# Filter stage with its sum and difference first and half the one-column products; two norms with the gate product ahead of the root, output written in halves

## What is computed

```python
def rmsnorm_2(x, g):
    return x * rsqrt(mean(x * x) + 1e-6) * g
def ffn_half(s, shift, scale, gate, g_pre, g_post, w_in, w_out):
    h = swiglu_2(modulate(rmsnorm_2(s, g_pre), shift, scale), w_in, w_out)
    return s + 0.5 * gate * rmsnorm_2(h, g_post)
# hyena_kernel, L = 256
h = h @ w4
h_fwd, h_bwd = split(h, 2)
h_fwd, h_bwd = h_fwd * decay, h_bwd * decay
k = concat([h_fwd, zeros, h_bwd[:0:-1]])
return k / (sum(abs(k), axis=0) + 1e-6)
# bidir_long_conv
y = irfft(rfft(u, 2 * L) * rfft(k, 2 * L))[:L]
# second_block
xs = ffn_half(xs, ...)
y = token_mixer(hx, ...)
xs = xs + mod_x[5] * rmsnorm_2(y, g[3])
return ffn_half(xs, ...)
```

## Time and profile before

| | |
|---|---|
| three executions | 2611.27, 2613.20, 2613.49 us |
| profiled execution, its own time | 2607.8 us |
| its span in the trace | 2606.0 us |
| mean granted clock of TensorE | 0.987 |
| TensorE busy | 2511.2 us (96%) |
| VectorE busy | 1811.8 us (70%) |
| ScalarE busy | 1451.3 us (56%) |
| share of TensorE in the chain that ended last | 84% |

### The profile page before, as it was taken

The page is one execution under the profiler, slowest core; times in us unless marked ns, Lnnn a source line. Parts: engine busy times, 40 slices in busy tenths (PEclk is TensorE's granted clock), DMA queues, the critical chain, the costliest instruction groups (busy, mean ns, idle before and its releaser), DMA issues.

```text
span 2606.0 us, 33172 instructions
## 1 busy us (share of the span) xinstructions
PE 2511.2 (96%) x11783; PEld 1992.0 (76%) x11783; DVE 1811.8 (70%) x1759; ACT 1451.3 (56%) x1613; POOL 67.0 (3%) x54
## 2 busy tenths in 40 slices
PE   7989999989999999999999999999999999998998
PEld 6668887667888888888888777888874787777787
DVE  6555446558999998989898985655544575777554
ACT  4553434547777777777777775435332333466443
POOL 0000000011000000000000000600000000000000
PEclk9999999989999999999999999999999999999999
DMA  6885552759999999999999996655534334435651
GB/s 218 308 285 189 192 178 81 266 175 378 394 373 358 370 364 367 354 375 347 381 351 377 340 342 204 232 183 187 184 129 138 101 126 146 125 104 172 203 190 65
DMA packets 330622, 642.13 MB, mean 246 GB/s; under 512 B 14408, under 2 KB 113256, under 8 KB 330344
## 3 DMA queue, kind: packets, MB, share of 16 engines
q1 hardware_dynamic: 327800, 631.02, 69.6%
q0 software_dynamic: 2736, 9.96, 1.0%
HBM read 633.07 MB, written 7.86 MB: 246 GB/s over the span
## 4 chain that ended last, share of the span: by engine, by line
PE 84%; DVE 7%; ACT 4%; issue 3%; DMA 1%; POOL 0%; SPq 0%; DVEq 0%; ACTq 0%; POOLq 0%
PE ps L926 19%; PE ps L852 19%; PE ps L956 10%; PE ps L881 10%; PE ps L1335 6%; PE ps L786 5%; PE ps L1362 2%; PE ps L1267 2%; DVE As L2343 1%; PE ps L1070 1%; ACT As L1736 1%; PE ps L865 1%; PE ps L941 1%; PE ps L1326 1%; DVE ringL L2313 1%
## 5 line engine op out<-in xcount | busy, mean ns | idle before, releaser
L2343 DVE TENSOR_TENSOR As<-ringA,As 128x2048 fp32r<-128x2048 f32 x318 | 733.7, 2308 | 220.3 <-ACT As L1653 132.4
L926 PE MATMUL ps<-As,xgs 128*128 128x512 f32 x2688 | 660.4, 395 | 6.4 <-DVE As L2343 3.8
L926 PEld LDWEIGHTS ps<-As,xgs 128*128 128x128 f32 x2688 | 494.7, 188 | 112.7 <-issue 5.7
L1736 ACT ACTIVATE As<-ringA 128x2048 fp32r<-128x2048 f32 x224 | 428.7, 1914 | 29.9 <-PE ps L926 27.6
L852 PE MATMUL ps<-As,xs 128*128 128x512 f32 x1456 | 376.0, 396 | 3.9 <-DVE hh L2380 3.9
L956 PE MATMUL ps<-Bs,hds 128*128 128x512 f32 x1332 | 323.4, 391 | 5.0 <-DVE hds L2406 2.2
L852 PEld LDWEIGHTS ps<-As,xs 128*128 128x128 f32 x1456 | 273.0, 190 | 63.4 <-DVE hh L2380 4.8
L956 PEld LDWEIGHTS ps<-Bs,hds 128*128 128x128 f32 x1332 | 248.0, 188 | 64.2 <-issue 11.0
L2425 DVE TENSOR_TENSOR Bs<-ringB,Bs 128x2048 fp32r<-128x2048 f32 x111 | 254.1, 2289 | 7.7 <-ACT Bs L1766 5.2
L1766 ACT ACTIVATE Bs<-ringB 128x2048 fp32r<-128x2048 f32 x111 | 213.2, 1921 | 63.0 <-PE ps L956 62.3
L881 PE MATMUL ps<-Bs,hds 128*128 128x512 f32 x1056 | 247.9, 390 | 0.0
(11 more groups left out here) (399 smaller groups left out, 3246.0 us busy)
## 6 DMA issues: line engine op xcount, KB each, us to landing
ringA<-in_moe_w_gate SPq DMA_DIRECT2D x112, 1024.0 KB, 5.9
ringA<-in_moe_w_up SPq DMA_DIRECT2D x112, 1024.0 KB, 6.1
ringB<-in_moe_w_down SPq DMA_DIRECT2D x112, 1024.0 KB, 6.1
ringA<-in_w_ff_in SPq DMA_DIRECT2D x132, 512.0 KB, 4.7
ringA<-in_w_in SPq DMA_DIRECT2D x56, 1024.0 KB, 5.3
ringA<-in_w_ada SPq DMA_DIRECT2D x36, 1024.0 KB, 6.4
ringB<-in_w_ff_out SPq DMA_DIRECT2D x33, 1024.0 KB, 5.0
ringA<-in_dense_w_gate SPq DMA_DIRECT2D x28, 512.0 KB, 3.6
```

Of the source, the lines that this page charges most:

```text
L926: m = mm(ps[:, bank, :], lhs(l, tt, k), As[:, h, r, k % 4, :], start=k == 0 and n == 0, stop=k == KC - 1 and n == 2)
L1736: A(As[:, h, 0, :, :], ringA[:, (p["a"] + u) % 2, 4 * h:4 * h + 4, :], ACT.Copy).then_inc(A_high, 1)
L2343: V.tensor_tensor(As[:, h, 1, :, :], ringA[:, (p["a"] + u) % 2, 4 * h:4 * h + 4, :], f32(As[:, h, 0, :, :]), ALU.subtract).then_inc(A_spli ...
```

## The change

**Filter stage.** For tile 0 nothing changes. For tile 1 VectorE makes the sum (into `decay`) and the difference (into `ha[:, 1]`) right after `hs` and `hd`, and counts up `f_h` after each; the copy (L2909) falls away, the absolute values come after. TensorE goes to the transform at `f_h` = 2 (groups 4 to 7, which read the difference, at 3). The absolute values of both tiles are added on VectorE into `hs[:, 1]` between its copies 5 and 9, so the column sums are 8 one-column products in the place of 16, and they stand behind the transform. `rn` is read then; the second block of `z` waits for that. `late_high` and `weight_low` of the first block of `z` move between the copies.

**Norm after `wo`.** The product of each half with the gate (`mixed_gate`) is made as soon as that half is squared, without the reciprocal; one fused pass `x = xn * rr + x` (`mixed_add`) follows the root. For tile 1 that pass stands ahead of `split_rows(0)`.

**The end.** The last `down` finishes the first 512 columns of a tile ahead of the second (`down_halves`). Squares, gate products, final passes and output DMAs go by halves of 512 columns.

```diff
@@ SyncE
             for tt in range(TILES):
-                sp.wait_ge(x_out, tt + 1)
-                sp.dma_start(out[tt * P:(tt + 1) * P, :], x[:, tt, :]).then_inc(out_done, 16)
-            sp.wait_ge(out_done, 32)
+                for half in range(2):
+                    c = slice(half * BW, (half + 1) * BW)
+                    sp.wait_ge(x_out, 2 * tt + half + 1)
+                    sp.dma_start(out[tt * P:(tt + 1) * P, c], x[:, tt, c]).then_inc(out_done, 16)
+            sp.wait_ge(out_done, 64)
@@ TensorE
+                def down_halves(i, u, weights):
+                    for tt in range(T):
+                        pe.wait_ge(hdT_ready, ffn_count(p, T, e, i, u, tt))
...
+                        for half in range(2):
+                            for q in range(2):
+                                for n, (l, r) in enumerate(((0, 0), (0, 1), (1, 0))):
+                                    m = mm(ps[:, 4 + 2 * tt + half, :], hds[:, tt, l, q, :], weights[r][:, q, half * 512:(half + 1) * 512],
...
+                            m.then_inc(down_done if half else acc_half, 1)
...
             pe.wait_ge(f_h, 2)
-            for c in range(KC):
-                for tt in range(TILES):
-                    last = mm(ps[:, 3, c:c + 1], ha[:, tt, c * P:(c + 1) * P], ones[:, 0:1], start=tt == 0, stop=tt == TILES - 1)
-            last.then_inc(rn_mm, 1)
...
             for q in range(10):
                 fc, half = q // 2, q % 2
-                src = hd if fc in (2, 3) else hs
+                src = (hd[:, 0, :], ha[:, 1, :]) if fc in (2, 3) else (hs[:, 0, :], decay)
                 if q >= 4:
                     pe.wait_ge(k_copied, q - 3)
+                if q == 4:
+                    pe.wait_ge(f_h, 3)
...
+            pe.wait_ge(f_h, 4)
+            for c in range(KC):
+                last = mm(ps[:, 3, c:c + 1], hs[:, 1, c * P:(c + 1) * P], ones[:, 0:1], start=True, stop=True)
+            last.then_inc(rn_mm, 1)
             pe.wait_ge(k_copied, 10)
...
             for n in range(6):
+                if n == 1:
+                    pe.wait_ge(rn_read, 1)
@@ ScalarE
-            for h in range(2):
-                late_high(ph["z"], 0, h)
             for q in range(0, 10, 2):
...
                 A(KF[:, q // 2, 0:512], ps[:, 4 + q % 4, :], ACT.Copy).then_inc(k_copied, 1)
+                if q < 4:
+                    late_high(ph["z"], 0, q // 2)
...
             for tt in range(TILES):
+                act.wait_ge(acc_half, tt + 1)
+                A(fnrow[:, 0:BW], ps[:, 4 + 2 * tt, :], ACT.Square, accum_out=ss[:, tt:tt + 1]).then_inc(squared, 1)
+                act.wait_ge(squared, 2 * TILES + 2 * tt + 1)
+                ch.done(A(std[:, 2 + tt:3 + tt], ss[:, tt:tt + 1], ACT.Identity, scale=1.0 / D, bias=epsc[1e-6]))
                 act.wait_ge(down_done, ph["ff1"]["s"] + 2 * NB2 - 1 + tt)
-                ch.done(A(xn[:, tt, :], ps[:, 4 + 2 * tt:6 + 2 * tt, :].rearrange("p a b -> p (a b)"), ACT.Square, accum_out=ss[:, tt:tt + 1]))
-                A(std[:, tt:tt + 1], ss[:, tt:tt + 1], ACT.Sqrt, bias=epsc[1e-6], scale=1.0 / D).then_inc(fin_std, 1)
+                A(fnrow[:, 0:BW], ps[:, 5 + 2 * tt, :], ACT.Square, accum_out=ss[:, 2 + tt:3 + tt]).then_inc(squared, 1)
+                act.wait_ge(squared, 2 * TILES + 2 * tt + 2)
+                A(std[:, tt:tt + 1], ss[:, 2 + tt:3 + tt], ACT.Sqrt, bias=std[:, 2 + tt:3 + tt], scale=1.0 / D).then_inc(fin_std, 1)
@@ VectorE
+                if tt:
+                    V.tensor_tensor(decay, hs[:, 1, :], hd[:, 1, :], ALU.add).then_inc(f_h, 1)
+                    V.tensor_tensor(ha[:, 1, :], hs[:, 1, :], hd[:, 1, :], ALU.subtract).then_inc(f_h, 1)
+                    continue
...
+            for q in range(1, 10, 2):
+                wait((k_mm, q + 1), (k_copied, q))
+                V.tensor_copy(KF[:, q // 2, 512:D], ps[:, 4 + q % 4, :]).then_inc(k_copied, 1)
+                if q < 4:
+                    weight_low(ph["z"], 0, q // 2)
+                if q == 5:
+                    ch.done(V.tensor_tensor(hs[:, 1, :], hs[:, 1, :], hd[:, 1, :], ALU.add))
+                if q == 7:
+                    V.tensor_tensor(hs[:, 1, :], hs[:, 1, :], ha[:, 0, :], ALU.add).then_inc(f_h, 1)
...
-            mixed_out(0)
+            for n in range(2):
+                mixed_gate(0, n)
             mixed_add(0)
+            mixed_gate(1, 0)
             tile_scale("ff1", 0, x, 1)
             plain_rows(0)
-            mixed_out(1)
+            mixed_gate(1, 1)
+            mixed_add(1)
             split_rows(0)
-            mixed_add(1)
             A_parts(ph["ff1"], 0, 0, 0, 1)
...
             for tt in range(TILES):
+                for half in range(2):
+                    c = slice(half * BW, (half + 1) * BW)
+                    dve.wait_ge(squared, 2 * TILES + 2 * tt + half + 1)
+                    V.tensor_tensor(xn[:, tt, c], ps[:, 4 + 2 * tt + half, :], gateG[:, 3, c], ALU.mult).then_inc(gated, 1)
                 dve.wait_ge(fin_std, tt + 1)
                 ch.done(V.reciprocal(rr[:, tt:tt + 1], std[:, tt:tt + 1]))
-                ch.done(V.scalar_tensor_tensor(xn[:, tt, :], acc(tt), rr[:, tt:tt + 1], gateG[:, 3, :], ALU.mult, ALU.mult))
-                V.tensor_tensor(x[:, tt, :], x[:, tt, :], xn[:, tt, :], ALU.add).then_inc(x_out, 1)
+                for half in range(2):
+                    c = slice(half * BW, (half + 1) * BW)
+                    dve.wait_ge(gated, 2 * TILES + 2 * tt + half + 1)
+                    V.scalar_tensor_tensor(x[:, tt, c], xn[:, tt, c], rr[:, tt:tt + 1], x[:, tt, c], ALU.mult, ALU.add).then_inc(x_out, 1)
```

More of the change, by code:

```diff
@@ L813, in project, with feed @@
                         between()
-            def feed(p, lhs, T, e=0, ready=None, xsm=None, after=None, head=1, leads=True, drains=True, rows=None, turns_free=None):
+            def feed(p, lhs, T, e=0, ready=None, xsm=None, after=None, head=1, leads=True, drains=True, rows=None, turns_free=None, halves=False):
                 nb = p["nb"]
@@ L900, in body @@
                         down(*prev, tts=(1,))
-                        down(i, u, weights=down_home(p, p["b"] + u))
+                        (down_halves if halves else down)(i, u, weights=down_home(p, p["b"] + u))
                     elif not lead:
@@ L1510, in _ @@
                 turn_rows("ff1", 0, hf)
-            feed(ph["ff1"], split_stream, 2, rows="ff1")
+            feed(ph["ff1"], split_stream, 2, rows="ff1", halves=True)
         @block.gpsimd
@@ L2909, in _ @@
                 V.tensor_copy(hs[:, tt, :], decay).then_inc(f_h, 1)
+            wait((f_h, 3))
+            V.scalar_tensor_tensor(hd[:, 1, :], hd[:, 1, :], -1.0, hd[:, 1, :], ALU.mult, ALU.max)
+            ch.done(V.scalar_tensor_tensor(hs[:, 1, :], hs[:, 1, :], -1.0, hs[:, 1, :], ALU.mult, ALU.max))
+            for h in range(2):
+                wait((xh_high, h + 1))
+                V.tensor_tensor(hTR[:, 4 * h:4 * h + 4, :], hT[:, 4 * h:4 * h + 4, :], f32(hcTR[:, 4 * h:4 * h + 4, :]), ALU.subtract).then_inc(xh_low, 1)
+            for q in range(1, 10, 2):
[7 more added lines that the diff above has]
+                    V.tensor_tensor(hs[:, 1, :], hs[:, 1, :], ha[:, 0, :], ALU.add).then_inc(f_h, 1)
             wait((rn_mm, 1))
@@ L2913, in _ @@
             ch.done(V.reciprocal(rn, rn))
-            for h in range(2):
-                wait((xh_high, h + 1))
-                V.tensor_tensor(hTR[:, 4 * h:4 * h + 4, :], hT[:, 4 * h:4 * h + 4, :], f32(hcTR[:, 4 * h:4 * h + 4, :]), ALU.subtract).then_inc(xh_low, 1)
-            for h in range(2):
-                weight_low(ph["z"], 0, h)
-            for q in range(1, 10, 2):
-                wait((k_mm, q + 1), (k_copied, q))
-                V.tensor_copy(KF[:, q // 2, 512:D], ps[:, 4 + q % 4, :]).then_inc(k_copied, 1)
+            dve.sem_inc(rn_read, 1)
             w = lambda j, c: vcol[:, 1, 24 * j + c:24 * j + c + 1]
@@ L3089, in _, with mixed_gate, mixed_add @@
             A_parts(ph["ff1"], 0, 0, 0, 0)
-            def mixed_out(tt):
+            def mixed_gate(tt, n):
+                c = slice(n * BW, (n + 1) * BW)
+                dve.wait_ge(squared, 2 * tt + n + 1)
+                V.tensor_tensor(xn[:, tt, c], ps[:, 4 + 2 * n + tt, :], gateG[:, 2, c], ALU.mult).then_inc(gated, 1)
+            def mixed_add(tt):
                 dve.wait_ge(wo_std, tt + 1)
                 ch.done(V.reciprocal(rr[:, 2 + tt:3 + tt], std[:, tt:tt + 1]))
-                for n in range(2):
-                    c = slice(n * BW, (n + 1) * BW)
-                    last = V.scalar_tensor_tensor(xn[:, tt, c], ps[:, 4 + 2 * n + tt, :], rr[:, 2 + tt:3 + tt], gateG[:, 2, c], ALU.mult, ALU.mult)
-                ch.done(last)
-            def mixed_add(tt):
-                V.tensor_tensor(x[:, tt, :], x[:, tt, :], xn[:, tt, :], ALU.add).then_inc(x_mixed, 1)
+                dve.wait_ge(gated, 2 * tt + 2)
```

(1 more changed line is left out.)

15 lines of the change are left out of this document (10 added, 5 removed).

## The result

The changed kernel takes 2600.76 us in the median of 8 executions (2595.59 to 2604.63), against 2613.61 us (2611.24 to 2618.78) for the kernel before in the executions beside it. The ratio is 0.9943, 95% interval 0.9932 to 0.9955. It is faster, as forecast, but by 12.9 us between medians where 8.1 were forecast, and the time lies 0.7 us under the range's lower end, 2601.5. By the prediction's own signs, a move of over 12 us counts against it.

The account below looks back on a forecast made before the run. TensorE was taken to bound the kernel, 84% of the chain that ended last. Terms -8.4 + 1.6 + 0.3 - 0.9 - 0.7 = -8.1 us, from a median of 2613.2 to 2605.1 us; range 2601.5 to 2608.5.

Parts of the forecast that it names:

- the prediction's own signs: Prediction wrong if transform shows gaps, `z` waits for sum of absolute values, or time moves under 5 or over 12 us.
- Filter stage, -8.4 us: Context tile's end to `z`: idle 2.34 us goes, transform at full clock, 16 records of one-column products: 8.4 us less.
- The clock behind it, +1.6 us: At `z`'s start: one-column products directly ahead bring the clock down, one fall costing 1.6 us.
- The bound of 0: Lower bound for the clock's cost at `z`'s start: no fall; the other bound was one fall, 1.6 us.
- the first rival: No fall: one-column products ahead of `z` do not bring the clock down; -9.7 us, 2603.5 us, chance 0.35.
- From `wo` to `ff1`, +0.3 us: TensorE starts 0.6 us later on tile 0's low part, tile 1's 0.24 us wait vanishes: 0.3 us more.
- The end, -1.6 us: After TensorE's last product: VectorE's passes done 0.9 us sooner, last output DMA by halves 0.7 us less.
- The given-back case: Behind `z`: falls of the clock land elsewhere, or the end wins nothing; -4.9 us, 2608.3 us, chance 0.13.
- the slower one: Filter stage: VectorE's copies behind `z`'s load-dependent low weights stop the transform; 2619.6 us if they land at 48, chance 0.03.

Follow-up runs that it names:

- filled kernels: Kernel before and changed kernel, each with eleven f32 products of constants in four TensorE idle times behind `z`: medians 2609.08 us and, over 12 executions together, 2596.6 us.
- plain pair: Changed kernel against the kernel before, both without added products of constants, one profiled execution each: spans 2599.2 and 2606.0 us.

## Why the prediction was wrong

Two steps failed, both about the clock. The fall behind the one-column products, +1.6 us in the sum, did not come. And the half clock in the old filter stage was priced from one execution, 1.5 us below what four of five traces show. Two smaller terms were off by 0.7 and 0.3 us.

**Filter stage, -8.4 us: right in its steps.** The idle time went, the transform takes 17.17 us (17.2 said), nothing is late in VectorE's queue, and `z` waits for nothing. The products took 1.68 us, not 1.9. The gain against the profiled execution was 8.6 us. But the low clock was read from a single execution. "2.2 less than now" for the transform and 5.00 us for the products are what one placing of the fall gave; in four of five traces with the old stage it cost 1.5 us more. The step that failed is the pricing of a clock fall that differs between executions as if it were a fixed duration: the stage gains 10.3 us in most traces. The reading behind it, that the clock fell because of the one-column products, rests on that same trace; in the other four the clock was at half when they began or within 0.3 us of it.

**The clock behind it, +1.6 us: wrong.** "I take the fall" rested on the low clock at 30.4 to 33.0, where the products came on top of 2.34 us of idleness. Eight products alone, 1.68 us, were followed by no fall in any of eight traces of the new stage; sixteen alone were, in the one trace that has them. The bound of 0 was the right value, and the first rival (2603.5 us) the right case. The Trainium skill (TensorE: Matmul & The Clock Gate, The HAM clock gate) puts the clock down to how busy the engine has been recently. The traces agree, with 0.50 behind idle times such as the 2.35 us of the old stage. That the clock also fell to 0.50 in sixteen one-column products without idle time is shown by this case alone.

**From `wo` to `ff1`, +0.3 us: wrong in sign.** The wait for the low part grew by 0.45 us, near the 0.6 said. The wait of the transposes was taken at the 0.24 us that half clock left of it. When the first group runs at full clock it is 1.8 us without the part and 1.0 with it, in the filled kernels, so there the part gains 0.4 us. Only where the first group ran at half clock did the wait vanish. The plain pair shows 0.9 us more, with the low clock over all of the group and not over a part.

**The end, -1.6 us: 1.9 measured.** VectorE was done 3.0 us after the last product (3.4 said), the DMA's part was right: 2.7 to 2.0 us. The 0.6 us beside that term in the prediction comes from a fit that the Trainium skill (DMA: Bandwidth & Descriptors, Anatomy of one DMA) gives for GpSimd's path, and this transfer is on SyncE's queue. As an estimate by that fit the half would land in 2.6 us; it took 2.0, so only the difference is near.

**The sum.** Put right, these terms give -10.3 - 0.4 - 1.9 = -12.6 us where the forecast had -8.1. That is close to the 12.9 us of the result; the remaining 1.7 of the 14.3 us between all medians is not accounted for. The range was too narrow at its lower end, since the level of the median and the clock's part in the old stage both come from executions that were not seen, and it allowed 2 us for them. The given-back case, for which the upper end stood, does not show, nor did the slower one happen: VectorE's queue never held the transform up.

## What to carry to other kernels

Before a duration is taken from one trace, look at the clock in that stretch. Where it was down, the same stretch took another time in the next execution here (28.1 us once, 29.5 to 29.7 four times), and a wait of 0.24 us was one of 1.8 us that half clock hid. A busy TensorE is no proof of a full clock: eight one-column products behind the transform were free of a fall in eight traces, and sixteen were not in the one that has them. Where an execution's total spreads over ten us, compare a change by its stretches, with the falls around it removed in both kernels: that gave 12.5 us behind the last context product in one pair of traces, where the plain pair gave 10.8 there and 6.8 between its spans.

## What was not expected

The kernel before spreads over 19 us (2604.7 to 2623.8 us in 85 executions) with TensorE's mean granted clock between 0.981 and 0.990, and the part up to the filter stage alone varies by 14 us over the 14 traces. Eleven useless products make the kernel before 5.7 us faster by medians, and the changed one 3.9.
